# Both parts of the activations in one 512-column matmul for the feed-forward up product

## What is computed

```python
h = rmsnorm_2(x, norm_ffn_pre[l])
u = causal_depthwise_conv_2(h @ w_ffn_up[l], ffn_conv_w[l], ffn_conv_b[l])   # 3 taps over the tokens
u_gate, u_val = jnp.split(u, 2, axis=-1)                                     # 2816 columns each
y = (jax.nn.gelu(u_gate, approximate=True) * u_val) @ w_ffn_down[l]
x = x + rmsnorm_2(y, norm_ffn_post[l])
```

## Time and profile before

| | before |
|---|---|
| time, three runs | 1035.68, 1034.59, 1034.98 us |
| median | 1034.98 us |
| span of the profiled execution | 1035.6 us, 0.6 above the median |
| TensorE busy | 1006.8 us (97%) |
| VectorE busy | 678.0 us (65%) |
| ScalarE busy | 549.1 us (53%) |
| GpSimd busy | 85.3 us (8%) |
| mean granted TensorE clock | 0.988 of 2.4 GHz |

### The profile page before, as it was taken

The page is one execution under the profiler, slowest core; times in us unless marked ns, Lnnn a source line. Parts: engine busy times, 40 slices in busy tenths (PEclk is TensorE's granted clock), DMA queues, the critical chain, the costliest instruction groups (busy, mean ns, idle before and its releaser), DMA issues.

```text
span 1035.6 us, 16582 instructions
## 1 busy us (share of the span) xinstructions
PE 1006.8 (97%) x6746; PEld 916.5 (88%) x6746; DVE 678.0 (65%) x991; ACT 549.1 (53%) x804; POOL 85.3 (8%) x104
## 2 busy tenths in 40 slices
PE   8999999999999989999999999989999989999997
PEld 7998899999987856899999999979999879999996
DVE  4969565554557688475555565478665749877775
ACT  6897454444446477554444453256554446555452
POOL 2710010000002210020000000000003310000000
PEclk9999999999999999999999999989999989999999
DMA  9736595556535624566555547444453625655531
GB/s 310 231 121 206 167 319 202 172 192 200 167 120 184 223 63 167 178 204 202 179 186 193 176 144 218 137 128 132 134 157 136 237 68 182 226 176 203 169 116 41
DMA packets 120308, 180.42 MB, mean 174 GB/s; under 512 B 3145, under 2 KB 93609, under 8 KB 120249
## 3 DMA queue, kind: packets, MB, share of 16 engines
q1 hardware_dynamic: 118384, 174.11, 51.1%
q0 software_dynamic: 1536, 5.36, 1.5%
q10 hardware_dynamic: 329, 0.12, 0.0%
HBM read 178.48 MB, written 1.10 MB: 173 GB/s over the span
## 4 chain that ended last, share of the span: by engine, by line
PE 89%; DVE 6%; ACT 2%; issue 1%; DMA 1%; SPq 0%; POOL 0%; DVEq 0%; POOLq 0%; ACTq 0%
PE PS L1085 45%; PE PS L1130 29%; PE PS L1119 2%; DVE wlo L1665 2%; PE PS L1323 2%; PE PS L1280 2%; PE PS L1420 2%; PE PS L1569 1%; DVE arena L1770 1%; PE PS L1402 1%; PE PS L1371 1%; PE PS L1104 1%; DMA arena<-in_norm_mem 1%; PE PS L1355 1%; PE PS L1352 1%
## 5 line engine op out<-in xcount | busy, mean ns | idle before, releaser
L1085 PE MATMUL PS<-XA,whi 128*128 128x256 f32 x2480 | 454.2, 285 | 0.3 <-DVE wlo L1665 0.3
L1665 DVE TENSOR_TENSOR wlo<-raw,whi 128x2048 fp32r<-128x2048 f32 x154 | 354.5, 2306 | 143.7 <-ACT whi L633 143.2
L1085 PEld LDWEIGHTS PS<-XA,whi 128*128 128x128 f32 x2480 | 391.4, 193 | 6.1 <-issue 1.9
L633 ACT ACTIVATE whi<-raw 128x2048 fp32r<-128x2048 f32 x153 | 291.7, 1909 | 141.4 <-PE PS L1130 101.6
L1085 PE MATMUL PS<-XA,wlo 128*128 128x256 f32 x1240 | 351.8, 284 | 0.0
L1085 PEld LDWEIGHTS PS<-XA,wlo 128*128 128x128 f32 x1240 | 238.8, 193 | 0.0
L1130 PE MATMUL PS<-whi,XB 128*128 128x512 f32 x736 | 209.3, 391 | 0.0
L1130 PEld LDWEIGHTS PS<-whi,XB 128*128 128x128 f32 x736 | 135.6, 188 | 26.6 <-issue 0.5
L1130 PE MATMUL PS<-wlo,XB 128*128 128x512 f32 x368 | 117.5, 390 | 0.0
L1130 PEld LDWEIGHTS PS<-wlo,XB 128*128 128x128 f32 x368 | 69.1, 188 | 14.6
L822 ACT ACTIVATE arena<-PS 128x256 f32<-128x256 f32 x64 | 24.2, 383 | 96.2 <-PE PS L1085 95.7
(11 more groups left out here) (234 smaller groups left out, 1134.9 us busy)
## 6 DMA issues: line engine op xcount, KB each, us to landing
raw<-in_w_up SPq DMA_DIRECT2D x32, 1024.0 KB, 5.4
raw<-in_w_down SPq DMA_DIRECT2D x32, 1024.0 KB, 5.0
raw<-in_w_ffn_up SPq DMA_DIRECT2D x22, 1024.0 KB, 5.1
raw<-in_w_in SPq DMA_DIRECT2D x21, 1024.0 KB, 5.3
raw<-in_w_ffn_down SPq DMA_DIRECT2D x11, 1024.0 KB, 4.9
raw<-in_w_kv SPq DMA_DIRECT2D x8, 1024.0 KB, 5.0
raw<-in_a_w_in SPq DMA_DIRECT2D x7, 1024.0 KB, 7.3
raw<-in_w_mem_kv SPq DMA_DIRECT2D x4, 1024.0 KB, 5.2
```

The costliest lines, as they stand in the source:

```text
L633: act.activation(whi[:, s, :], raw[:, s, :], ACT.Copy).then_inc(s_hi, 1)
L1085: ins = pe.matmul(PS[:, bank_of(g), 0:T], w[:, k, P * m:P * m + P], X[:, k0 + k, part, :], start=(i == 0 and part == 0 and w is hi), stop= ...
L1665: dve.tensor_tensor(wlo[:, s, :], raw[:, s, :], whi[:, s, :].bitcast(F32), ALU.subtract).then_inc(s_lo, 1)
```

## The change

In the feed-forward part alone, the high weights are multiplied with both parts of the activations in one matmul of 512 columns; the product with the low part lands in the second half of the bank. The low weights still meet the high activations in a matmul of 256 columns, into the first half. A tile k thus has two matmuls in place of three. ScalarE copies the second half of the bank to `fu` (`ffn_low`, semaphore `s_fb`), VectorE adds the first half of the bank to it in place (`s_evac`), and GpSimd multiplies it with `rstd_row` in place (`s_fu`). tap2 waits for GpSimd. ScalarE's order becomes: split of u + 3; the two copies of e = 0; split of u + 4; tap2 of e = 0; the two copies of e = 1; gelu; tap2 of e = 1; split of u + 5; the high part. `first_up` in step 0 and `up2_` in all steps call `both_parts` and `group_both` in place of the three matmuls. VectorE's order is as before, with adds in place of the multiplications.

```diff
@@ GpSimd
+            pool.wait_ge(s_row, 2)
+            for g in range(4 * FFN_STEPS):
+                pool.wait_ge(s_evac, G_FFN + g + 1)
+                v = fu[:, g % 4, 2:2 + T]
+                pool.tensor_tensor(v, v, rstd_row[:], ALU.mult).then_inc(s_fu, 1)
@@ ScalarE
-                    act.wait_ge(s_evac, g0 + m + 1)
+                    act.wait_ge(s_fu, g0 - G_FFN + m + 1)
...
+            def ffn_low(u, e, j):
+                if j:
+                    act.wait_ge(s_conv2, 2 * j + e - 1)
+                for m in range(2):
+                    act.wait_ge(s_step, BEFORE(u + e) + m + 1)
+                    act.activation(fu[:, 2 * e + m, 2:2 + T], PS[:, bank_of(G_FFN + 4 * j + 2 * e + m), T:2 * T], ACT.Copy)\
+                       .then_inc(s_fb, 1)
...
                 split(u + LEAD)
+                ffn_low(u, 0, j)
+                split(u + 1 + LEAD)
                 if j:
                     act.wait_ge(s_fl, j)
                 ffn_tap2(G_FFN + 4 * j, 0, j)
-                split(u + 1 + LEAD)
+                ffn_low(u, 1, j)
                 act.wait_ge(s_conv2, 2 * j + 1)
                 act.activation(fc[:, 0:2, :], fc[:, 0:2, :], ACT.Gelu_apprx_tanh).then_inc(s_gelu2, 1)
                 ffn_tap2(G_FFN + 4 * j + 2, 1, j)
@@ TensorE
+            def both_parts(bank, hi, lo, x, opens, closes):
+                pe.matmul(PS[:, bank, :].rearrange("p (e n) -> p e n", e=2), hi, x, start=opens, stop=False,
+                          skip_group_check=True)
+                return pe.matmul(PS[:, bank, 0:T], lo, x[:, 0, :], start=False, stop=closes, skip_group_check=True)
+
+            def group_both(g, slot, m, it, groups):
+                pe.wait_ge(s_evac, it * groups + g - ring_of(g) + 1)
+                hi, lo = W8(whi, slot), W8(wlo, slot)
+                for i, k in enumerate(KO):
+                    ins = both_parts(bank_of(g), hi[:, k, P * m:P * m + P], lo[:, k, P * m:P * m + P], XA[:, k],
+                                     i == 0, i == KT - 1)
+                ins.then_inc(s_step, 1)
...
@@ VectorE
-                    if j == 0 and e == 0:
-                        dve.wait_ge(s_row, 2)
                     for m in range(2):
                         g = G_FFN + 4 * j + 2 * e + m
-                        dve.wait_ge(s_step, BEFORE(u + e) + m + 1)
-                        dve.tensor_tensor(fu[:, 2 * e + m, 2:2 + T], PS[:, bank_of(g), 0:T], rstd_row[:], ALU.mult)\
-                           .then_inc(s_evac, 1)
+                        v = fu[:, 2 * e + m, 2:2 + T]
+                        dve.wait_ge(s_fb, g - G_FFN + 1)
+                        dve.tensor_tensor(v, PS[:, bank_of(g), 0:T], v, ALU.add).then_inc(s_evac, 1)
```

More of the change, by code:

```diff
@@ L332, in bass_blocks @@
         s_tanh = sem("branch_gates")
+        s_fb, s_fu = sem("ffn_low_part"), sem("ffn_up_normed")
         s_ssf = sem("sumsq_ffn")
@@ L1105, in res_T, with first_up @@
                 ins.then_inc(s_xnT, 1)
-            def first_up(u, g, n, second_half):
+            def first_up(u, g, n, second_half, both=False):
                 have(u)
@@ L1117, in first_up @@
                     for m in range(2):
[L1118 to L1121, removed]
+                        at = slice(P * m, P * m + P)
+                        if both:
+                            ins = both_parts(bank_of(g + m), hi[:, k, at], lo[:, k, at], XA[:, k], k == 0, k == KT - 1)
+                        else:
+                            for w, part in ((hi, 0), (hi, 1), (lo, 0)):
+                                ins = pe.matmul(PS[:, bank_of(g + m), 0:T], w[:, k, at], XA[:, k, part, :],
+                                                start=(k == 0 and part == 0 and w is hi), stop=(k == KT - 1 and w is lo),
+                                                skip_group_check=True)
                         if k == KT - 1:
@@ L1605, in up2_ @@
                 if j == 0:
-                    first_up(u, G_FFN, 6, ffn_second_half)
+                    first_up(u, G_FFN, 6, ffn_second_half, both=True)
                     have(u + 1)
-                    group(G_FFN + 2, (u + 1) % SLOTS, 0, W8, KT, XA)
+                    group_both(G_FFN + 2, (u + 1) % SLOTS, 0, 0, 0)
                     pe.wait_ge(s_rstd, ROOTS[SQ_NORM[6]] + TT)
@@ L1614, in up2_ @@
                     ins.then_inc(s_bc, 1)
-                    group(G_FFN + 3, (u + 1) % SLOTS, 1, W8, KT, XA)
+                    group_both(G_FFN + 3, (u + 1) % SLOTS, 1, 0, 0)
                 else:
-                    unit_a(u, G_FFN + 4 * j)
-                    unit_a(u + 1, G_FFN + 4 * j + 2)
+                    for e in range(2):
+                        have(u + e)
+                        for m in range(2):
+                            group_both(G_FFN + 4 * j + 2 * e + m, (u + e) % SLOTS, m, 0, 0)
             def down2(j):
```

## The result

| | before | after |
|---|---|---|
| median | 1035.33 us (4 runs, 1034.59 to 1036.27) | 1046.65 us (4 runs, 1044.26 to 1049.10) |
| ratio | | 1.0115, 95% interval 1.0098 to 1.0132 |
| span of the profiled execution | 1035.6 us | 1047.3 us |
| TensorE, VectorE, ScalarE, GpSimd busy | 1006.8, 678.0, 549.1, 85.3 us | 1008.5, 685.4, 562.2, 157.7 us |

The kernel became 11.3 us slower. The forecast was 1035.4 and the range went up to 1041; the time is that of the second rival, 1047, which I had given one chance in ten.

What follows compares the result with a forecast made beforehand. TensorE was taken as the bound, VectorE's loop (15.8 us) staying under its 16.60 us step. Matmuls -4.2, first step +2.95, last step +1.6 gave +0.4 on 1034.98: 1035.4 us, range 1031.3 to 1041.

Steps and rivals of the forecast that it cites:

- the second rival: Split gets the port whenever issued first: halves 4.66 us, loop 17.0, TensorE waits every step from down(1): 1047, chance 0.10.
- What bounds the kernel: Feed-forward steps: TensorE, 97% busy, 16.98 us a step, is the bound as long as VectorE keeps below TensorE's step.
- the 0.8 us a step: After the late first step, VectorE gains 0.8 us a step until a group's arrival times the adds.
- The term of 4.2 us: Up products: a tile falls from 0.3598 to 0.3478 us, 0.012 less, over 352 tiles.
- Who goes first at the port: Shared SBUF port, weight split against GpSimd's second multiply: GpSimd keeps it, 4.02 us from first add to conv2, loop 15.8.
- the 804 rows: Earlier profile: split issued at 804.00, 0.35 us into a GpSimd op; GpSimd's next op went first, the split took 3.26.
- the 812 rows: Earlier profile: split issued at 812.63 during a GpSimd op went first; GpSimd's next op waited, 2.79 us for 0.74.
- First step: Step 0 to down(1): 1.95 us lost ahead of down(0), plus evacuation and weight waits; losses sum to 2.96.
- Last step: End of the stage: last low part done at 1024.68, down(10) starts at 1024.7, 1.6 us lost.
- The third rival: Clock drops to 0.50 behind the expected stalls ahead of down(0) or down(10): 1036.5 to 1037.1, both 1038.2; chance 0.20.
- The first: Rival: the port costs nothing, a half takes 2.9 us in place of 4.02: 1031.8, chance 0.18.
- the fourth: Rival: the wide matmul gives nothing, a pair takes 0.36 us: 1038.5, chance 0.10.

Runs made afterwards that it cites:

- the version with three matmuls: Changed kernel with three 256-column matmuls a tile again; copies, adds and GpSimd's multiplies stay: 1046.8 us, ratio 1.0108.
- the wide matmul alone: Kernel before plus the wide matmul, its low-activation product left out of the sum; no copies, adds or GpSimd multiplies: 1033.45 us, ratio 0.9978.
- the fill in their place: Kernel before, attention part: GpSimd's two loads ahead of the ninth branch add moved behind the adds, a 128x1365 fill put there: 1036.61 us (one run).
- the delayed split: Changed kernel with a fill of 0 to 512 columns, varied by step, and a wait between VectorE's second add and the split: 1042.76 us (one run).

## Why the prediction was wrong, point by point

- **What bounds the kernel.** Right for the kernel before, and the condition named with it, that VectorE's loop stay under TensorE's step, was the one that broke: 16.85 us against TensorE's 16.79. The condition itself was too weak, for the version with three matmuls keeps it (16.85 under 16.98) and loses as much; what the forecast needed were the 0.8 us a step that VectorE was to gain on TensorE, and it gained none.
- **What the matmuls give.** The mechanism is right, the size was off. The term of 4.2 us measured 2.3 us (the wide matmul alone, ratio 0.9978). I had added the pitches of two unbroken runs; in alternation a tile takes 0.353 us in the mean, every third one 0.36. With the widths kept apart it takes 0.349, near the 0.348 of the sum.
- **Who goes first at the port.** This step failed: "So I let GpSimd keep the port." The split went first in every pair where it was issued at once, the half took 4.56 us and not 4.02, the loop 16.85 and not 15.8. The four numbers compared (0.19 and 0.34 into the first operation against 0.35 and 0.50) were about right (0.17 and 0.32 were measured for the first two); what I overlooked is that the 804 rows had two loads issued just ahead of them, while the 812 rows, which went the other way, had not. With the fill in their place the same moment gave the opposite outcome. The experiment in which GpSimd is let go first gave 4.07 us for a half and 1.0022, which is what the forecast had described.
- **The rule of the Trainium skill.** I set its sentence that issue order decides ("SBUF — State Buffer", section "Who interferes with whom") aside on these rows. In the changed kernel the trace agrees with it: the split, issued while the second multiply had not yet been issued behind the first, went ahead at 0.51 us and held the port for its whole 2.28 us. With the delayed split it agrees too, if the second multiply counts as issued at its recorded start, 0.60 us after the first's, and not when its input was ready. The place at 804 us differs from it in all eleven traces.
- **First step.** Forecast: 1.95 us ahead of down(0), 0.47 for down(1)'s weights, 0.20 and 0.17 for evacuations. Measured: 2.15, 1.2, and 0.8 in two. Near for the first, since the low part there comes after two halves only; the others grew with the longer half.
- **Last step.** Forecast 1.6 us, measured 6.9: VectorE was behind, and not a group's arrival but its own order timed the last adds, as in the second rival. With the port given to GpSimd first, the waits ahead of down(0) and down(10) together were 2.8. The lower clock behind the long wait, 2.2 us, was not in the forecast's sum.
- **The sum.** Forecast: -4.2 + 2.95 + 1.6. Measured in the two traces: -2.3 for the matmuls, 4.2 of waits in the first steps, 0.5 between down(1) and down(9), 6.9 ahead of down(10), 2.2 by the clock, 11.5 together. Restarting behind the five waits took about 1.1 us more than the listed waits, and this trace reached the stage 0.9 earlier for reasons outside the change; with both it is the 11.7 between the spans.
- **Rivals.** The second one happened in its mechanism: the split first in each half, the loop (17.0 forecast, 16.85 measured), and a low part that comes late at the end. That its time was hit as well (1047 forecast, 1046.65) is in part luck. It put 0.4 us of waiting in every step, and there were 0.06; it put the last low part at about 1036.5, and it came at 1033.75; and it knew nothing of the 2.2 us by the clock that this trace has. Its point of decision, about 0.4 us more per half, was not measured: 0.54 more per half brought the loss, and a half of 4.07 us did not. Its chance of 0.10 was far too low for a mechanism that rested on one event against another. The third rival had the sign of a stall's consequence right at the end of the stage only: behind 6.9 us the clock fell (and behind 5.9 in the version with three matmuls), behind 2.15 it did not. The first and the fourth fell: the port cost 12 to 13 us, the pair was worth 2.3.

## What to carry to other kernels

Before work is moved to GpSimd, see which two-input VectorE instruction is issued right behind the producer: in these runs it took the port ahead of all but GpSimd's first operation, so a pair of short GpSimd operations cost a whole long one (3.38 us in place of 1.33). Let the long instruction wait for the short ones, even if this adds a wait. A rule for who goes first that is read at one place of a trace may hold for that place alone, even if it repeats there in every run: look at what else was going on in its neighbourhood, and give the other side its chance. And ask of a chain beside the bottleneck not only whether its loop is shorter, but whether it gains enough a step to make up a late start.

## What the runs showed of the hardware that I had not expected

- GpSimd lets go of the shared port before its recorded end and takes it anew for the next operation, though that one is ready: 0.51 us after the start for a multiply of 128x256 recorded as 0.64, 0.62 for an add recorded as 0.74.
- Two loads issued by GpSimd just ahead turned this round: a split took 3.26 us in place of 2.55, and so in all eleven traces that have the loads there. Why is open.
- Alternating 512- and 256-column matmuls cost 4 ns a pair in the mean over running each width in a row (0.353 against 0.349 us), all of it in every third pair (0.36).
- Of the waits in these traces 2.15 us ahead of 868.18 left the clock at 1.00, in the kernel before 1.99 us ahead of 50.94 was followed by 0.50: the length of a wait alone does not tell.
